# GLA decays and block middles in PSUM, twenty weight rests on GpSimd, seven taps in the GLA steps, gate chain behind the eviction

## The reference, cut to what matters

```python
u = rms_norm(h, m_pre)
p_all = u @ w_in
ya, buf_a = conformer_conv(p_all[..., OFF_A:OFF_B], ...)   # A
yb, s_b = gla_mixer(p_all[..., OFF_B:OFF_C], ...)          # B
yc, buf_c = short_conv(p_all[..., OFF_C:OFF_D], ...)       # C
q, k, v, logf = fox_project(p_all[..., OFF_D:N_IN], d_bf)  # D, forgetting attention
y = jnp.concatenate([ya, yb, yc, yd], axis=-1) @ w_out

def conformer_conv(pa, buf, conv_w, conv_b, ln_g, ln_b):
    val, gate = jnp.split(pa, 2, axis=-1)
    a = val * jax.nn.sigmoid(gate)
    xpad = jnp.concatenate([buf.astype(a.dtype), a], axis=1)
    y = causal_depthwise(xpad, conv_w) + conv_b            # 31 taps
    y = jax.nn.silu(layer_norm(y, ln_g, ln_b))

def gla_mixer(pb, state, w_a2, b_a, norm_g):
    log_a = jax.nn.log_sigmoid((a_lr @ w_a2 + b_a)) / GLA_TAU
    # in chunks of 64: b = cumsum(log_a); scores[t, s] = sum_k q k exp(b_t - b_s), s <= t
    y = o * jax.nn.silu(g)
```

## Time and profile before

| | us |
|---|---|
| median of 3 runs (1093.55 to 1095.01) | 1094.26 |
| the profiled execution | 1094.53 |
| its span from first to last instruction | 1092.7 |
| its PE busy | 1064.1 |
| its DVE busy | 705.6 |
| its ACT busy | 550.6 |
| its POOL busy | 274.5 |

### The profile page before, as it was taken

How to read it: one execution, slowest core, us unless ns; L and a number is a source line. 1 busy time by engine, 2 the same in 40 slices (tenths; PEclk the granted TensorE clock), 3 DMA queues, 4 the chain that set the end, 5 groups by cost and what they waited for, 6 DMA issues and landing times. The chain is left out here.

```text
span 1092.7 us, 24133 instructions
## 1 busy us (share of the span) xinstructions
PE 1064.1 (97%) x8956; PEld 1028.8 (94%) x8956; DVE 705.6 (65%) x1045; ACT 550.6 (50%) x887; POOL 274.5 (25%) x340
## 2 busy tenths in 40 slices
PE   6999999989999999999999999999899999999997
PEld 5999999988879999999999999998888899999997
DVE  5666644589995766654476665436999776666443
ACT  6544454554357644454474445446534675444542
POOL 3222221304504322220132223012053042222200
PEclk9999999999999999999999999999999999999999
DMA  7666677342726566656646666763426257656561
GB/s 269 207 186 180 179 222 232 98 155 79 232 78 196 155 193 180 184 166 187 188 127 203 180 180 188 232 186 117 139 79 209 79 190 217 180 179 176 178 181 53
DMA packets 63747, 186.92 MB, mean 171 GB/s; under 512 B 9515, under 2 KB 19763, under 8 KB 63539
## 3 DMA queue, kind: packets, MB, share of 16 engines
q1 hardware_dynamic: 63666, 185.81, 56.2%
HBM read 182.40 MB, written 3.38 MB: 170 GB/s over the span
## 5 line engine op out<-in xcount | busy, mean ns | idle before, releaser
L313 DVE TENSOR_TENSOR w_lo<-raw,w_hi 128x1024 fp32r<-128x1024 f32 (+1 forms) x316 | 411.1, 1306 | 332.0 <-ACT w_hi L303 331.8
L303 ACT ACTIVATE w_hi<-raw 128x1024 fp32r<-128x1024 f32 x336 | 342.9, 1026 | 283.0 <-PE ub L345 188.4
L343 PE MATMUL ub<-hg_hi,w_hi 128*128 128x264 f32 x960 | 278.7, 290 | 6.3 <-DVE proj L1315 6.3
L344 PE MATMUL ub<-hg_lo,w_hi 128*128 128x264 f32 x960 | 274.9, 286 | 0.0
L345 PE MATMUL ub<-hg_hi,w_lo 128*128 128x264 f32 x960 | 274.6, 286 | 0.0
L343 PE MATMUL ub<-act_hi,w_hi 128*128 128x264 f32 x704 | 200.5, 285 | 0.0
L345 PE MATMUL ub<-act_hi,w_lo 128*128 128x264 f32 x704 | 200.0, 284 | 0.0
L344 PE MATMUL ub<-act_lo,w_hi 128*128 128x264 f32 x704 | 199.1, 283 | 0.0
L343 PE MATMUL quad<-hg_hi,w_hi 128*128 128x264 f32 x688 | 196.4, 285 | 0.0
L344 PE MATMUL quad<-hg_lo,w_hi 128*128 128x264 f32 x688 | 194.9, 283 | 0.0
L345 PE MATMUL quad<-hg_hi,w_lo 128*128 128x264 f32 x688 | 194.8, 283 | 0.0
(11 more groups left out here) (252 smaller groups left out, 1314.4 us busy)
## 6 DMA issues: line engine op xcount, KB each, us to landing
raw<-in_w_gu SPq DMA_DIRECT2D x176, 512.0 KB, 4.1
raw<-in_w_dn SPq DMA_DIRECT2D x64, 512.0 KB, 4.1
raw<-in_w_in SPq DMA_DIRECT2D x44, 512.0 KB, 3.8
raw<-in_w_dn SPq DMA_DIRECT2D x32, 384.0 KB, 3.7
raw<-in_w_out SPq DMA_DIRECT2D x16, 512.0 KB, 3.7
pages<-in_cache_k SPq DMA_DIRECT2D x32, 128.0 KB, 3.3
pages<-in_cache_v SPq DMA_DIRECT2D x32, 128.0 KB, 3.1
con<-in_con SPq DMA_DIRECT2D x1, 1448.0 KB
```

Source lines behind the costliest of these rows:

```text
L303: eng.activation(w_hi[:, slot, 0:w], raw[:, slot, 0:w], ACT.Copy).then_inc(*sig("hi_ready", reps))
L313: eng.tensor_tensor(w_lo[:, slot, 0:w], raw[:, slot, 0:w], w_hi[:, slot, 0:w].bitcast(F32), ALU.subtract)\
L343: eng.matmul(out, a_hi, x_hi[:, k0 + k, :], start=(first and k == 0), stop=False)
L344: eng.matmul(out, a_hi, x_lo[:, k0 + k, :], start=False, stop=False)
```

## The change

It does seven things.

- The decays go to the PSUM bank `mb[3]`, one buffer for all levels; `level_decays(i)` now waits for keys i-1. ACT also copies the running sums to PSUM (`mids`), and exponents 2 to 7 take the block middles from there.
- POOL makes the rests of units 7 to 23 and of units 0 to 2 of phase out: twenty, before ten.
- The conformer's product `a_pad` moves from step 11 to step 8. Taps start in step 8; taps 0 to 6 add up in SBUF (`ymix`), tap 7 crosses over to PSUM.
- The taps are spread anew: seven of them in steps 8 to 11, one in 12, two in 13, and 21 from step 15 on (before: seven in steps 12 and 13, 24 from 15 on).
- The GLA gate's chain goes from step 4 to step 5 on DVE, behind the eviction of unit 4.
- The sigmoid of the conformer's gate goes to step 6 on ACT, the other gate becomes one SiLU in step 12, and DVE's multiplication for it is dropped. AV and BG swap their unit numbers.
- Waits follow: PE takes its rests from `rest_half` where POOL makes them, and transposes the values after keys 7.

```diff
-ALR, FG, BQ, BK, AG, BG, AV, BV, DQ, DKK, DVV, CC, CX, CB = 0, 1, 2, 3, 4, 6, 8, 10, 12, 14, 16, 18, 19, 22
+ALR, FG, BQ, BK, AG, AV, BG, BV, DQ, DKK, DVV, CC, CX, CB = 0, 1, 2, 3, 4, 6, 8, 10, 12, 14, 16, 18, 19, 22
-POOLED = tuple(range(14, 24))
-TAPS = {12: (0, 2), 13: (2, 7), 15: (7, 12), 16: (12, 16), 17: (16, 20), 18: (20, 23), 19: (23, 27), 20: (27, 31)}
+POOLED = [("in", n) for n in range(7, 24)] + [("out", n) for n in range(3)]
+TAPS = {8: (0, 1), 9: (1, 3), 10: (3, 5), 11: (5, 7), 12: (7, 8), 13: (8, 10), 15: (10, 14), 16: (14, 19), 17: (19, 23), 18: (23, 25), 19: (25, 28), 20: (28, 31)}
+TAPS_PSUM = TAPS[12][0]
+        decay, mids = mb[3][:, 0:TP], mb[2][:, 0:TP]
             def level_decays(l, i):
-                if i >= 3:
-                    after(l, b_kt=i - 2)
-                act.activation(lv[:, 2 + i % 2, :], lv[:, i % 2, :], ACT.Exp, scale=1 / GLA_TAU).then_inc(*sig("b_E"))
+                if i >= 2:
+                    after(l, b_kt=i - 1)
+                act.activation(decay, lv[:, i % 2, :], ACT.Exp, scale=1 / GLA_TAU).then_inc(*sig("b_E"))
                 if n == 5:
+                    level_decays(l, 1)
                     after(l, b_bc=2)
+                    act.activation(mids, bc[:, 0:TP], ACT.Copy).then_inc(*sig("b_bp"))
                     act.activation(eb[:, :], bc[:, :], ACT.Exp, scale=1 / GLA_TAU).then_inc(*sig("b_eb"))
-                    level_decays(l, 1)
-                if n == 8:
+                if n == 6:
                     act.preload_act_table(ACT.Sigmoid)
-                    after(l, proj=8)
+                    after(l, proj=6)
                     act.activation(proj[:, AG:AG + 2, :], proj[:, AG:AG + 2, :], ACT.Sigmoid).then_inc(*sig("a_sg"))
-                    act.activation(sg[:, :, :], proj[:, BG:BG + 2, :], ACT.Sigmoid).then_inc(*sig("b_sg"))
...
-                mid = b[:, :, 0, m - 1:m].to_broadcast([P, TP // (2 * m), m])
+                mid = at_mid[:, :, 0, m - 1:m].to_broadcast([P, TP // (2 * m), m])
...
-                                  lv[:, 2 + i % 2, :].unsqueeze(1).to_broadcast([P, 2 - first, TP]), ALU.mult).then_inc(*sig("b_kt"))
+                                  decay.unsqueeze(1).to_broadcast([P, 2 - first, TP]), ALU.mult).then_inc(*sig("b_kt"))
...
-                        y, x, w = taps_sum[:, c * TP:(c + 1) * TP], a_pad[:, c, t:t + TP], ...
+                        early, late = ymix[:, YA + c, 0:TP], taps_sum[:, c * TP:(c + 1) * TP]
+                        y, x, w = early if t <= TAPS_PSUM else late, a_pad[:, c, t:t + TP], ...
-                            out = ymix[:, YA + c, 0:TP] if t == TAPS_A - 1 else y
+                            out = late if TAPS_PSUM <= t < TAPS_A - 1 else early
...
-                if n == 4:
+                if n == 5:
                     after(l, b_z=1, b_sp=3)
                     log_sigmoid(l, la[:, :], mb[2][:, 0:NT], par[:, PAR["ba"]:PAR["ba"] + 1], soft[:, :], "b_la")
-                if n == 11:
-                    after(l, a_sg=1, a_z=1, proj=10)
+                if n == 8:
+                    after(l, a_sg=1, a_z=1, proj=8)
...
-                    after(l, b_sg=1)
-                    dve.tensor_tensor(sg[:, :, :], sg[:, :, :], proj[:, BG:BG + 2, :], ALU.mult).then_inc(*sig("b_gs"))
...
-                for n in POOLED:
-                    rest_halves(pool, l, n)
+                for phase, n in POOLED:
+                    rest_halves(pool, l, phase, n)
```

More of the change, by code:

```diff
@@ L263, in pooled, with pool_count @@
         def pooled(phase, idx):
-            return phase == "in" and idx in POOLED
-        def pool_count(idx):
-            return 2 * POOLED.index(idx) + 2
+            return (phase, idx) in POOLED
+        def pool_count(phase, idx):
+            return 2 * POOLED.index((phase, idx)) + 2
         def turn_before(lead):
@@ L277, in pooled_just_before @@
         def pooled_just_before(lead):
-            if lead["phase"] == "out":
-                return len(POOLED) if lead["index"] == 0 else 0
-            return 0
+            return len(POOLED) if lead["phase"] == "out" and lead["index"] == LEAD else 0
         def load_unit(eng, lead, reps):
@@ L287, in load_unit @@
             if lead["phase"] in ("in", "out") and pooled(*turn_before(lead)):
-                eng.wait_ge(*at(lead["layer"], "rest_half", pool_count(turn_before(lead)[1])))
+                eng.wait_ge(*at(lead["layer"], "rest_half", pool_count(*turn_before(lead))))
             else:
@@ L314, in rest_unit, with rest_halves @@
                .then_inc(*sig("split_done", reps, 1 + pooled_just_before(lead)))
-        def rest_halves(eng, l, n):
-            eng.wait_ge(S["hi_ready"], l * UNITS + PHASES["in"][0] + n + 1)
+        def rest_halves(eng, l, phase, n):
+            eng.wait_ge(S["hi_ready"], l * UNITS + PHASES[phase][0] + n + 1)
             for half in range(2):
@@ L357, in multiply_first @@
                     if k == 0:
-                        eng.wait_ge(S["split_done"], l * UNITS + PHASES[phase][0] + s + 1 + RING)
+                        if pooled(phase, s):
+                            eng.wait_ge(*at(l, "rest_half", pool_count(phase, s)))
+                        else:
+                            eng.wait_ge(S["split_done"], l * UNITS + PHASES[phase][0] + s + 1 + RING)
                     if s == 0:
@@ L565, in gla_tokens @@
             def gla_tokens(l):
-                after(l, proj=12)
+                after(l, proj=12, b_kt=7)
                 transposes(mb[2], proj[:, BV:BV + 2, :], "b_vT")
@@ L740, in mixer @@
                     if pooled("in", n):
-                        pe.wait_ge(*at(l, "rest_half", pool_count(n)))
+                        pe.wait_ge(*at(l, "rest_half", pool_count("in", n)))
                     else:
@@ L874, in mix @@
                 if n == 5:
+                    level_decays(l, 1)
                     after(l, b_bc=2)
+                    act.activation(mids, bc[:, 0:TP], ACT.Copy).then_inc(*sig("b_bp"))
                     act.activation(eb[:, :], bc[:, :], ACT.Exp, scale=1 / GLA_TAU).then_inc(*sig("b_eb"))
-                    level_decays(l, 1)
                 if 6 <= n <= 11:
                     level_decays(l, n - 4)
-                if n == 8:
+                if n == 6:
                     act.preload_act_table(ACT.Sigmoid)
-                    after(l, proj=8)
+                    after(l, proj=6)
                     act.activation(proj[:, AG:AG + 2, :], proj[:, AG:AG + 2, :], ACT.Sigmoid).then_inc(*sig("a_sg"))
-                    act.activation(sg[:, :, :], proj[:, BG:BG + 2, :], ACT.Sigmoid).then_inc(*sig("b_sg"))
+                    act.preload_act_table_set("natural_log_exp_and_others")
+                if n == 12:
+                    act.preload_act_table(ACT.Silu)
+                    after(l, proj=10)
+                    act.activation(sg[:, :, :], proj[:, BG:BG + 2, :], ACT.Silu).then_inc(*sig("b_sg"))
                     act.preload_act_table_set("natural_log_exp_and_others")
@@ L1074, in level_exponents @@
                     after(l, b_E=i - 2)
+                if i == 2:
+                    after(l, b_bp=1)
                 out = lv[:, i % 2, :]
                 if i == 7:
-                    b, out = (t.rearrange("p (n m) -> p n m", m=CH) for t in (bc[:, 0:TP], out))
-                    dve.tensor_tensor(out, b[:, :, CH - 1:CH].to_broadcast([P, TP // CH, CH]), b, ALU.subtract).then_inc(*sig("b_D"))
+                    b, ends, out = (t.rearrange("p (n m) -> p n m", m=CH) for t in (bc[:, 0:TP], mids, out))
+                    dve.tensor_tensor(out, ends[:, :, CH - 1:CH].to_broadcast([P, TP // CH, CH]), b, ALU.subtract).then_inc(*sig("b_D"))
                     return
                 m = LEVELS[i]
-                b, out = (t.rearrange("p (n two m) -> p n two m", two=2, m=m) for t in (bc[:, 0:TP], out))
-                mid = b[:, :, 0, m - 1:m].to_broadcast([P, TP // (2 * m), m])
+                b, at_mid, out = (t.rearrange("p (n two m) -> p n two m", two=2, m=m) for t in (bc[:, 0:TP], mids if i > 1 else bc[:, 0:TP], out))
+                mid = at_mid[:, :, 0, m - 1:m].to_broadcast([P, TP // (2 * m), m])
                 dve.tensor_tensor(out[:, :, 0, :], mid, b[:, :, 0, :], ALU.subtract).then_inc(*sig("b_D"))
@@ L1107, in conv_taps @@
                         k = 2 * t + c
-                        y, x, w = taps_sum[:, c * TP:(c + 1) * TP], a_pad[:, c, t:t + TP], par[:, PAR["acw"] + c * TAPS_A + t:PAR["acw"] + c * TAPS_A + t + 1]
+                        early, late = ymix[:, YA + c, 0:TP], taps_sum[:, c * TP:(c + 1) * TP]
+                        y, x, w = early if t <= TAPS_PSUM else late, a_pad[:, c, t:t + TP], par[:, PAR["acw"] + c * TAPS_A + t:PAR["acw"] + c * TAPS_A + t + 1]
                         if t == 0:
-                            after(l, b_msk=7)
+                            after(l, a_in=1)
```

(10 more changed lines are left out.)

## The result

| | before | after |
|---|---|---|
| median, us | 1094.3 (1093.55 to 1095.01, 4 runs) | 1110.09 (1105.59 to 1110.75, 4 runs) |
| ratio after/before | | 1.0132, 95% interval 1.0116 to 1.0148 |
| profiled execution, its span | 1094.53, 1092.7 | 1110.65, 1108.8 |
| mean granted TensorE clock | 0.993 | 0.983 |

The change makes the kernel 1.3% slower. The forecast was 1106.0 with a range of 1085 to 1112. In short: POOL's new rests hold DVE in two places, PE waits behind both, and in layer 0 the clock takes some 5 us on top.

What follows compares the result with a forecast made beforehand. PE, busy 97% of the span, was taken as the bound, leaving its waits and low-clock stretches. 7.5 - 1.1 - 0.5 = +5.9 us a layer, +11.8 in all, gave a median of 1106.0, range 1085 to 1112.

Steps and rivals of the forecast that it cites:

- Turns between POOL and DVE: DVE instructions with two SBUF inputs take turns with POOL's, each costing up to one half of 1.25 us.
- The gate's chain behind the eviction: Steps 3 to 5: POOL's rests hold the forget gate's chain, so the stall moves from unit 6 to level 0.
- +0.8: Level 1 starts at 239.2 against 238.37, behind mask 0 and the slow unit 6: 0.8 us later.
- Step 8: Product, its decoded tail and tap 0 wait for POOL's rests 11 and 12: 3.8 us held in all.
- Steps 9 to 13: Taps and products wait for POOL's rests: 0.5, 2.0, 1.1, 2.4 and 2.0 us held, step by step.
- the turns are rarer: Rival: PE's stalls shift POOL's rests beside masks and keys; +0.9 us a layer, 1096, up to 1099; partly hidden, chance 0.15.
- My lower bound of 6.4: Between the evictions of units 7 and 13, at least 6.4 us of POOL's seven rests hold DVE.
- +7.5 at unit 15: Unit 15 waits for the late eviction of unit 13: +7.5 us a layer, the 0.8 included, at least +2.5.
- Last tap, -1.1: Later steps: DVE is ahead at the last tap, so PE's wait there goes, -1.1 us a layer.
- Transposes, -0.5: Step 22: the wait ahead of the transposes goes with DVE's and ACT's lateness, -0.5 us a layer.
- +5.9 a layer: Whole kernel: the sum 7.5 - 1.1 - 0.5 for each layer, +11.8 us in all.
- Slower by more: Rival: clock drops one unit more behind level 4, 1.6 us a layer, 1107 to 1110; chance 0.53 shared with the forecast.

Runs made afterwards that it cites:

- reads_beside: Before, plus four POOL subtractions reading constants into an unused tile once unit 7 is rounded; 1102.36 us, ratio 1.0079.
- writes_beside: Before, plus ten POOL memsets into an unused tile once unit 7 is rounded; 1098.33 us, ratio 1.0036.
- taps_first: After, with POOL starting the rests of units 11 to 16 only behind the step's taps or products; 1097.41 us, ratio 1.0035.
- gate_only: Before, with only the GLA gate's chain moved from step 4 to step 5 on DVE; 1096.05 us, ratio 1.0004.
- waits_and_late: After, with POOL's rest of unit 7 behind the exponents of level 1 and the taps where before had them; 1091.21 us, ratio 0.9964.
- late_and_yield: `waits_and_late`, with POOL also waiting behind the product, value products, `qe` and `st_tmp` (rests 11, 15, 16, 17); 1091.01 us, ratio 0.9976.

## Why the prediction was right, point by point

- **Turns between POOL and DVE**, the term said to decide: right, shown by `reads_beside` without the change. A TENSOR_SCALAR is held, as I took it from the copy of the earlier trace rows; `writes_beside` shows it apart.
- **The gate's chain behind the eviction**: right in each step. Eviction of unit 3 at 233.65 forecast, 233.13 measured; level 0 at 234.0 and 233.69; unit 6 at 234.45 and 234.11; the half clock behind it stays; "+0.8" at level 1 is +0.3 at unit 7. "The stall isn't removed, it moves" is what the rows of after show.
- **Step 8**: held 3.8 forecast, 3.5 measured (product 0.5 over that of `taps_first`, its tail 1.1, tap 0 2.0). The wait of level 4: 3.4 forecast, 2.7 and 2.8 measured.
- **Steps 9 to 13**: 8.0 forecast before the overlap; 6.9 in layer 1 and 4.4 in layer 0. The evictions of units 7 and 13 are 29.4 and 26.9 us apart, where I had 31.4; DVE's work unheld is 19.0 of that, not 19.8. In layer 1 the rests came where I had put them:

```profile
804.01 3.73 DVE L1129 SCALAR_TENSOR_TENSOR yg<-a_pad,par,yg 128x256 f32<-128x256 f32 x4
...
808.94 3.00 DVE L1129 SCALAR_TENSOR_TENSOR yg<-a_pad,par,yg 128x256 f32<-128x256 f32 x4
...
804.32 2.75 POOL L321 TENSOR_TENSOR w_lo<-raw,w_hi 128x512 fp32r<-128x512 f32 x2 [3.58 <-ACT w_hi L303]
808.15 2.71 POOL L321 TENSOR_TENSOR w_lo<-raw,w_hi 128x512 fp32r<-128x512 f32 x2 [1.09 <-ACT w_hi L303]
```

  Four taps take 1.66 us unheld (first row below), so steps 10 and 11 are held 2.1 and 1.3, where I had 2.0 and 1.1. Step 9 has 0.3 for 0.5, step 12 2.1 for 2.4 and step 13 1.1 for 2.0. In layer 0 steps 10 and 11 read:

```profile
256.56 1.66 DVE L1129 SCALAR_TENSOR_TENSOR yg<-a_pad,par,yg 128x256 f32<-128x256 f32 x4
...
259.42 2.70 DVE L1129 SCALAR_TENSOR_TENSOR yg<-a_pad,par,yg 128x256 f32<-128x256 f32 x4
...
258.32 2.73 POOL L321 TENSOR_TENSOR w_lo<-raw,w_hi 128x512 fp32r<-128x512 f32 x2 [5.04 <-ACT w_hi L303]
...
257.18 1.06 ACT L303 ACTIVATE w_hi<-raw 128x1024 fp32r<-128x1024 f32 x1 [3.90 <-PE ub L345]
```

  The stall ahead of level 4 is in both layers, the half clock behind it only in this one. It delays the end of unit 10 and with it the rounding of unit 14; POOL idles for 5.04 us, and the taps of step 10 run free. This is what the rival "the turns are rarer" had said: stalls that shift the rests. My count took PE at full speed in unit 10. In steps 8 to 13 layer 0 is held 8.0 us in all and layer 1 10.4, where I had 11.6. My lower bound of 6.4 took 2.4 us for each of the seven rests where the text has 2.5; with 2.5 it is 7.1, and layer 0 is near it.
- **+7.5 at unit 15**: the term that was mis-sized. It measured +4.56 and +5.65. In layer 0 it is PE's own lateness since level 4 (unit 11 is already at +4.55); DVE's later lateness is covered by it. In layer 1 PE's waits ahead of levels 4, 5 and 6 are 2.79, 0.25 and 1.94, where I had 3.4, 0.7 and 2.0, and unit 15 is no later than unit 14, where I had 0.6 more for the eviction of unit 13.
- **Last tap, -1.1**: right; unit 22 gains 1.34 on unit 21 in both layers.
- **Transposes, -0.5**: wrong. The wait on `smT` is 1.1 in two as in the earlier trace rows, and the one on `yg` is 1.4 in two for 0.5; unit 23 loses 0.9 on unit 22 in layer 1. I took for granted that a PE that is late finds everything done; DVE is late by as much. By how much each of its last instructions adds to that wasn't tried.
- **The clock**: in neither sum. My total of +5.9 a layer is met in layer 1 (+5.55), where too high a term at unit 15 and a gain that did not come make up for each other, which is luck, and missed by 5 in layer 0 (+10.95). "Slower by more" gave 1107 to 1110 and the median is 1110.1, but only one part of its mechanism is there: the drop behind level 4 occurs in layer 0 alone, and the larger part comes in steps 15 to 20, from stretches that no row before level 4 announces.

So the sign and most of the size rest on the mechanism that was forecast. With layer 1's +5.55 in both layers the profiled execution would be at 1105.6.

## What to carry to other kernels

Work moved to GpSimd isn't free for VectorE: list VectorE's instructions with two SBUF inputs, and its copies and TENSOR_SCALARs within SBUF, in every stretch where GpSimd would run; a tiny one costs up to a whole instruction of GpSimd's, and a chain of four small ones cost 3.5 us here. Give GpSimd a place in the order (a wait behind the chain) instead of leaving it to start when its data is there: one wait took away the first stall, and a wait for each of six rests nearly all of the second. And a stall that is moved in front of another consumer is no gain; ask what waits next, as `gate_only` shows.

## What the runs showed of the hardware that I had not expected

- The same wait of PE doesn't always bring the half clock. Ahead of level 4 it idles 2.68 us in layer 0 and 2.79 in layer 1 of one execution; behind it the granted clock is 0.50 in the first and 1.00 in the second (windows above).
- The clock also falls where PE has not been idle. Before has one such drop in each layer, behind a stretch in which small matmuls keep PE busy throughout:

```profile
275.80:279.20 3.40, 3.40 (x55) 2.98 (x56) 3.30 (x11) 0.89 (x1) 0.00 (x0) 1.00 0.43 152
279.25:282.55 3.30, 3.30 (x17) 3.30 (x16) 2.96 (x8) 0.73 (x4) 2.52 (x2) 0.50 0.65 156
```

  In after the one of layer 0 comes at 282.69 and lasts 6.83 us. Two more follow, at 299.76 and 310.00. They begin in runs of the attention's small matmuls, which again keep PE busy (3.41 of 3.41 us ahead of 299.71), as the timeline of PE shows:

```profile
298.97 0.70 PE L628 MATMUL quad<-proj,qm 128*128 128x256 f32 x2
299.60 1.10 PE L629 MATMUL quad<-y_sq,con 4*128 4x256 f32 x2
...
301.02 0.42 PE L344 MATMUL ub<-hg_lo,w_hi 128*128 128x264 f32 x1
```

  A matmul of 264 columns is 0.42 us there against 0.28. The same matmuls in layer 1, and in before, bring no drop at this place. What decides stays open: no run here changes that alone. It is worth some 5 us in one layer, and most of the spread inside `waits_and_late` goes with it (1099.4 at a mean clock of 0.983, the six others from 1089.3 to 1092.3 at 0.994 to 0.996); where it comes often it gives back what was won in the levels: 3.3 us a layer at unit 14 became 1.9 by unit 23 in `late_and_yield` and a loss of 2.9 in `waits_and_late`.
- An instruction of VectorE on 4 partitions is held as long as one on 128: the product of 4x264 takes 1.40 us where it took 0.42, and each half of tap 0, 128x256, 1.36 to 1.44 where `taps_first` has 0.41.
